# Attention items of a hybrid trunk: sample heads in pairs, past keys as stationary operand, five items ahead in place of three

## What is computed

```python
def sb_attend(q_pos, q, k, v, k_pos):
    z = jnp.einsum('bhqd,bhkd->bhqk', q, k) * (HEAD_DIM ** -0.5)
    mask = k_pos[None, :] < q_pos[:, None]
    log_skip = jnp.where(mask, jax.nn.log_sigmoid(-z), 0.0)
    later = lax.cumsum(log_skip, axis=3, reverse=True) - log_skip
    w = jnp.where(mask, jnp.exp(jax.nn.log_sigmoid(z) + later), 0.0)
    return jnp.einsum('bhqk,bhkd->bhqd', w, v)

def fox_attend(q_pos, q, fq, k, v, k_pos, fk):
    z = jnp.einsum('bhqd,bhkd->bhqk', q, k) * (HEAD_DIM ** -0.5)
    z = z + fq[..., :, None] - fk[..., None, :]
    z = jnp.where(k_pos[None, :] <= q_pos[:, None], z, -jnp.inf)
    return jnp.einsum('bhqk,bhkd->bhqd', jax.nn.softmax(z, axis=-1), v)
```

## Time and profile before

| | |
|---|---|
| median of 3 runs | 1691.65 us (1691.54 to 1693.9) |
| profiled execution | 1690.64 us |
| its span | 1688.5 us |
| PE busy over the span | 1509.1 us (89%) |
| DVE, ACT busy | 932.9 us (55%), 779.2 us (46%) |
| items stage, first to last matmul | 634 to 994 us |
| mean granted TensorE clock | 0.95 |

### The profile page before, as it was taken

How to read it: one execution, slowest core, us unless ns; L and a number is a source line. 1 busy time by engine, 2 the same in 40 slices (tenths; PEclk the granted TensorE clock), 3 DMA queues, 4 the chain that set the end, 5 groups by cost and what they waited for, 6 DMA issues and landing times. The chain is left out here.

```text
span 1688.5 us, 23869 instructions
## 1 busy us (share of the span) xinstructions
PE 1509.1 (89%) x8837; PEld 1343.5 (80%) x8837; DVE 932.9 (55%) x1169; ACT 779.2 (46%) x1109; POOL 187.4 (11%) x135
## 2 busy tenths in 40 slices
PE   5799999999999989999999989979964998999950
PEld 3479899999999978888999979967853876878840
DVE  7623012222323327777777744443246997999947
ACT  8422012113332327777777741121113776787733
POOL 0100000000000002000000001212103333432320
PEclk9899999999999999999999989989976999999985
DMA  7246344547656659776657223444316899999538
GB/s 282 82 128 193 110 141 145 168 150 218 205 186 184 213 174 233 186 200 152 152 126 178 72 101 106 162 146 162 113 50 200 249 335 300 261 280 288 105 53 323
DMA packets 233077, 300.14 MB, mean 178 GB/s; under 512 B 86441, under 2 KB 171537, under 8 KB 232954
## 3 DMA queue, kind: packets, MB, share of 16 engines
q1 hardware_dynamic: 223458, 264.01, 51.2%
q0 software_dynamic: 9504, 34.61, 8.5%
HBM read 264.23 MB, written 87.81 MB: 208 GB/s over the span
## 5 line engine op out<-in xcount | busy, mean ns | idle before, releaser
L773 PE MATMUL G<-hhi,proj_whi 128*128 128x384 f32 x768 | 178.5, 340 | 0.0
L773 PE MATMUL G<-hhi,proj_wlo 128*128 128x384 f32 x768 | 176.1, 337 | 0.0
L773 PE MATMUL G<-hlo,proj_whi 128*128 128x384 f32 x768 | 176.0, 337 | 0.0
L2005 DVE TENSOR_TENSOR experts_ulo<-plain,experts_uhi 128x2048 fp32r<-128x2048 f32 x66 | 150.8, 2285 | 18.9 <-issue 10.3
L1109 PE MATMUL G<-items_WT,items_vt 128*128 128x128 f32 x1152 | 150.6, 276 | 0.3
L1949 ACT ACTIVATE experts_uhi<-plain 128x2048 fp32r x66 | 126.6, 1920 | 33.8 <-PEq L80 23.4
L1109 PEld LDWEIGHTS G<-items_WT,items_vt 128*128 128x128 f32 x1152 | 139.4, 192 | 2.0 <-ACT items_WT L1162 2.0
L773 PEld LDWEIGHTS G<-hhi,proj_whi 128*128 128x128 f32 x768 | 136.0, 188 | 2.7 <-DVE proj_wlo L853 2.2
L773 PEld LDWEIGHTS G<-hhi,proj_wlo 128*128 128x128 f32 x768 | 137.8, 188 | 0.0
L773 PEld LDWEIGHTS G<-hlo,proj_whi 128*128 128x128 f32 x768 | 137.7, 188 | 0.0
L1906 PE MATMUL G<-experts_uhi,experts_ghi 128*128 128x512 f32 x264 | 109.0, 413 | 9.1 <-DVE experts_glo L2009 8.7
(11 more groups left out here) (314 smaller groups left out, 3157.9 us busy)
## 6 DMA issues: line engine op xcount, KB each, us to landing
plain<-in_w_dram SPq DMA_DIRECT2D x132, 512.0 KB
plain<-in_w_dram SPq DMA_DIRECT2D x33, 1024.0 KB
proj_wraw<-in_w_ada_dram SPq DMA_DIRECT2D x32, 512.0 KB
proj_wraw<-in_w_in_dram SPq DMA_DIRECT2D x20, 512.0 KB
qkhi_d<-proj_ohi SPq DMA_DIRECT2D x16, 576.0 KB, 2.8
qklo_d<-proj_olo SPq DMA_DIRECT2D x16, 576.0 KB, 3.0
gate_d<-proj_full SPq DMA_DIRECT2D x16, 576.0 KB, 3.8
merge_sg<-gate_d SPq DMA_DIRECT2D x16, 576.0 KB, 6.2
```

What stands on the lines that cost most here:

```text
L773: m = pe.matmul(G[:, g + c, 0:CH], w[r][:, k, :], a[:, k, c * CH:(c + 1) * CH], start=k == 0 and q == 0, stop=k == KD - 1 and q == 2)
L2005: dve.tensor_tensor(half(ulo[j], c), raw_up(side[n], c), half(uhi[j], c).bitcast(F32), ALU.subtract).then_inc(u_lo, 1)
```

## The change

Scores of the sample item's past part are turned round: each sequence's past keys `kc` are stationary and its queries move, high and low side by side in 32 columns, from a joint tensor `q` (`qs` in the code). That is eight matmuls and gives keys by queries, high and low apart. `add_past` on DVE adds the two into `zt` in two operations, and PE transposes `zt` into the slot (`turn_past`). `widen`, `qmhi` and `qmlo` are gone. Values of the sample item are computed once for two heads of the same kind: `take` writes both heads' weights to `W2`, and the second head's values handle 256 columns and 32 columns a sequence. `AHEAD` is 5, `S` has six buffers, `R` four, and y is split one item later. PE's first wait is for the first diagonal mask.

```diff
-                AHEAD = 3
+                AHEAD = 5
+                RING = 4
...
-                    pe.wait_ge(masks, FIRST_MASK)
+                    pe.wait_ge(masks, DIAGONAL)
...
                             for b in range(NB):
-                                for j, qm in enumerate((qmhi, qmlo)):
-                                    pe.matmul(G[:, g, 0:P], qm[:, b * P:(b + 1) * P], kc[f][:, b * PAST:(b + 1) * PAST],
-                                              start=b == 0 and j == 0, stop=b == NB - 1 and j == 1)
-                            m = part(G[:, g, P:2 * P], ks[f][:, SEQ:T], mnew[f])
-                        m.then_inc(z_ready, 1)
+                                new = slice(SEQ + b * NQ, SEQ + (b + 1) * NQ)
+                                m = pe.matmul(G[:, g + 1, b * 2 * NQ:(b + 1) * 2 * NQ], kc[f][:, b * PAST:(b + 1) * PAST], qs[f][:, :, new],
+                                              start=True, stop=True)
+                            m.then_inc(z_past, 1)
+                            part(G[:, g, P:2 * P], ks[f][:, SEQ:T], mnew[f])
+
+                    def turn_past(n):
+                        pe.wait_ge(z_summed, n // TT + 1)
+                        pe.transpose(G[:, slot(n), 0:P], zt[:], ident[:]).then_inc(z_ready, 1)
...
+                            out = G[:, 4 + y % 2, 0:2 * P]
+                            pe.matmul(out, vt[f][:, TT - 1, :], W2[f][:, 1].rearrange("p e n -> p (e n)"), start=True, stop=False)
+                            pair = out.rearrange("p (e n) -> p e n", e=2)
                             for b in range(NB):
-                                m = pe.matmul(out[:, b * NQ:(b + 1) * NQ], vc[f][:, b, :], w[:, 0, b * NQ:(b + 1) * NQ],
-                                              start=False, stop=b == NB - 1)
+                                new = slice(b * NQ, (b + 1) * NQ)
+                                m = pe.matmul(pair[:, :, new], vc[f][:, b, :], W2[f][:, 0, :, new], start=False, stop=b == NB - 1)
...
-                        if 0 <= i - 1 < NI:
+                        if 0 <= i - 1 < NI and has_pv(i - 1):
                             values(i - 1)
+                        if 0 <= i + AHEAD < NI and late(i + AHEAD):
+                            turn_past(i + AHEAD)
...
+                    def add_past(n):
+                        parts = G[:, slot(n) + 1, 0:2 * P].rearrange("p (b j i) -> p b j i", j=2, i=NQ)
+                        if n >= TT:
+                            dve.wait_ge(z_ready, n - TT + 1)
+                        dve.wait_ge(z_past, n // TT + 1)
+                        dve.tensor_copy(zt[:].rearrange("p (b i) -> p b i", i=NQ), parts[:, :, 0, :]).then_inc(z_first, 1)
+                        dve.wait_ge(z_first, n // TT + 1)
+                        dve.tensor_tensor(zt[:].rearrange("p (b i) -> p b i", i=NQ), parts[:, :, 1, :], zt[:].rearrange("p (b i) -> p b i", i=NQ),
+                                          ALU.add).then_inc(z_summed, 1)
...
+                    for i in range(-AHEAD, NI + 2):
+                        if 0 <= i + AHEAD < NI and late(i + AHEAD):
+                            add_past(i + AHEAD)
+                        if 0 <= i + AHEAD - 1 < NI and items[i + AHEAD - 1][0] == 0:
+                            stick(i + AHEAD - 1)
+                        if 0 <= i + AHEAD < NI and items[i + AHEAD][0] == 1 and not late(i + AHEAD):
+                            least(i + AHEAD)
+                        if 0 <= i + AHEAD - 1 < NI and items[i + AHEAD - 1][0] == 1:
+                            invert(i + AHEAD - 1)
+                        if 0 <= i + AHEAD < NI and items[i + AHEAD][0] == 1 and late(i + AHEAD):
+                            least(i + AHEAD)
+                        if 0 <= i - 2 < NI and y_last(i - 2):
+                            low_y(i - 2)
```

More of the change, by code:

```diff
@@ L1062, in part @@
                         def part(out, key, mask):
-                            pe.matmul(out, qhi[f][:, q], key, start=True, stop=False)
+                            pe.matmul(out, qs[f][:, 0, q], key, start=True, stop=False)
                             if mask is not None:
@@ new lines, in high_y @@
+                        for e in both if late(n) else (h % 2,):
+                            a, t0, w = slice(e * HD, (e + 1) * HD), t // 4 * 4, (t % 4 + 1) * P
+                            first = e * P if late(n) else 0
+                            act.activation(yhi[a, 4 * f + h // 2, t0 * P:t0 * P + w], G[a, 4 + y_use(n) % 2, first:first + w], ACT.Copy).then_inc(y_hi, 1)
+                    act.wait_ge(masks, FIRST_MASK)
+                    for i in range(-AHEAD, NI + 2):
+                        if 0 <= i + AHEAD - 1 < NI and items[i + AHEAD - 1][0] == 1:
+                            exponent(i + AHEAD - 1)
+                        if 0 <= i + AHEAD < NI and items[i + AHEAD][0] == 0 and not late(i + AHEAD):
+                            weigh(i + AHEAD)
@@ L1237, in _ @@
[L1237 to L1247 removed]
+                        dve.wait_ge(y_hi, y_done[y_use(n) + 1])
@@ new lines, in low_y @@
+                        for e in both if late(n) else (h % 2,):
+                            a, t0, w = slice(e * HD, (e + 1) * HD), t // 4 * 4, (t % 4 + 1) * P
+                            first = e * P if late(n) else 0
+                            dve.tensor_tensor(ylo[a, c, t0 * P:t0 * P + w], G[a, 4 + y_use(n) % 2, first:first + w],
+                                              yhi[a, c, t0 * P:t0 * P + w].bitcast(F32), ALU.subtract).then_inc(y_lo, 1)
+                    dve.wait_ge(masks, FIRST_MASK)
```

136 lines of the change are left out of this document (53 added, 83 removed).

## The result

The changed kernel takes 1720.26 us (median; 1717.12 to 1721.63), the kernel before 1692.49 on the same chip. The ratio is 1.0165 with a 95% interval of 1.0151 to 1.0179: slower by 28 us. The prediction said slower, 1706 in a range of 1668 to 1722. The direction was right, the size of the loss was about half of what came.

What follows compares the result with a forecast made beforehand. PE was taken to bound the kernel, with DVE and ACT no reserve. Five ahead was to lose the sample part's saving: 1690.6 + 14.7 for the heads + 1.0 to the median, rounded 1706 us, range 1668 to 1722.

Steps and rivals of the forecast that it cites:

- What bounds the kernel: Items stage: PE sets the pace, busy 325.2 of 332.6 us; DVE and ACT not full, but no reserve.
- Parts 1 and 2: Sample scores turned round and sample values paired on PE: 13.3 and 14.9 us saved, 28.2 if nothing else is late.
- Part 3: Small edits: copies and memsets hidden, add_past 0.55 us a head on DVE, earlier first scores under 1 us.
- Part 4, stick heads: Five ahead: PE waits for add_past's sum, a least and a take; 24.3 us, 24.9 with paired values, before 23.18.
- The walk: Round-by-round adding of PE, DVE and ACT steps through a head, giving PE's waits: 5.55 us in an unpaired stick head.
- Part 4, FoX heads: Five ahead: waits for add_past's sum and behind ACT's table load; 21.55 us, 22.85 with paired values, before 21.53.
- Head 0: Start of the loop, already DVE's chain, with add_past now in it: about +2 us (0 to 3).
- Head 15: Last head, no later scores and no table switch: 1.3 us saved.
- The sum: Heads 2 to 13 +12.5 us, head 14 +1.1, head 15 -1.3, head 0 +2, last y copies +0.4: +14.7.
- The signs: PE waits 1.5 to 3 us for add_past's sum in stick heads; wrong if under 1, or FoX heads average below 20.
- The saving arrives: Rival: PE's saving shows because DVE reaches add_past by 6.6 us; 1655 to 1687 us, chance 0.22.
- The clock falls too: Rival: PE's clock drops after its 2.6 us stand in stick heads; 1714 to 1722 us or beyond, chance 0.15.

Runs made afterwards that it cites:

- Kernel 1: Changed kernel with three items ahead, two R buffers and y one item later, so the new sample part alone: 1690.7 us, 0.9992 of the kernel before.
- kernel 6: Changed kernel with AHEAD 3, ACT's take ahead of the sigmoid's table load and its y copy first in the round: 1668.7 us, ratio 0.9861.
- kernel 3: Changed kernel, five ahead, with ACT copying y at the start of its round, not at its end: 1705.8 us, ratio 1.0101.
- kernel 4: Changed kernel with 12 unread PE transposes per stick head (28 in head 0) before the wait for add_past's sum: 1714.1 us, ratio 1.0131.
- kernel 7: Changed kernel, five ahead, with both ACT order changes (take before the sigmoid's table load, y copy first): 1698.0 us, ratio 1.0042.
- kernel 5: Kernel before with its old sample part, given only five ahead, four R buffers and the later y: 1720.7 us, ratio 1.0164.
- kernel 2: Changed kernel, five ahead, with ACT doing the take before the sigmoid's table load in a head's first item: 1706.6 us, ratio 1.0087.
- kernel 12: As kernel 6 (three ahead, both ACT order changes) but with two R buffers in place of four: 1667.9 us, ratio 0.9850.
- kernel 9: Kernel 6 with the pairing undone, each head's sample values computed apart: 1678.2 us, ratio 0.9915.

## Why the prediction was right or wrong, step by step

**What bounds the kernel.** PE set the pace before, and DVE and ACT are no reserve: held. Kernel 1 shows it best: 17.7 us less busy time on PE, as much more waiting, and no time gained.

**Parts 1 and 2.** Eight matmuls of 32 columns appear as x8 with 1.04 us including the tail and 0.89 to the next row (787.53 to 788.42 in head 6), 0.111 from start to start where 0.107 were taken; the sum of PE's work without waits, 18.77 a FoX head, was measured as 18.9 (kernel 6). Paired values 2.15 and not 2.0. Sizes right within 0.2 us a head.

**Part 3.** `add_past` was taken at 0.55 us: COPY 0.28 and the sum 0.29, 0.53 from the start of the first (791.67) to the start of the next scan (792.20). Right. PE's first wait, for the mask, is 8.2 us in place of 9.2.

**Part 4, stick heads.** Forecast 24.3 and 24.9, measured 24.31 and 25.28. The walk's places are all there: the sum last, then the least at item 2 of the next head, then the take behind the exponent. Their sizes are not those of the walk: 0.59 + 0.41 + 2.14 = 3.14 in place of 4.05 up to the sum, 0.73 in place of 1.05, 0.36 in place of 0.45: 4.23 in all where the walk had 5.55. PE's busy time made up for it: 20.07 us in this head by the first row below (the stretch of head 6), where 18.77 were taken. So the exact 24.31 is luck: two errors of 1.3 us cancel. Why PE is busy longer for the same work when it stops in between is not shown; the row's duration is longer than the step from one start to the next, and behind each stop that tail is counted too.

```profile
780.20:804.50 24.30, 20.07 (x157) 17.55 (x156) 17.71 (x29) 16.82 (x34) 0.00 (x0) 1.00 0.44 105
804.50:828.20 23.70, 21.39 (x175) 19.59 (x174) 16.10 (x36) 16.24 (x37) 0.00 (x0) 1.00 0.66 160
```

**Part 4, FoX heads.** Forecast 21.55 and 22.85, measured 21.91 and 23.71. The waits of the second are 23.7 - 21.39 = 2.3 us in all (second row), against 2.05 forecast; the busy time is 21.4 against 20.8. This is a term of the walk that was mis-sized, and more in PE's work than in its waits: 0.86 a head, with the 0.36 of the other FoX head and the 0.38 of the paired stick head 1.6 in four heads, 4.8 in heads 2 to 13.

**The clock.** Here the prediction failed as a sum. It saw the drop in a row, priced it (4 heads x 2.4, up to 10), and gave it a chance of 0.15 as a rival, with nothing for it in the forecast, when it comes on top of the forecast. The heads in which the clock fell are 4, 10, 11 and 13; they were 0.69, 1.28, 1.61 and 1.63 us longer than their like, 5.2 in all. Of head 4's 0.69, 0.35 is not the clock's: kernels 3, 4 and 7, granted 1.00 there, have head 4 longer than head 8 by the same 0.35. That leaves 4.9 for the clock, and in kernel 4, with the wait filled, it is gone. The rival put the drops into stick heads, behind the wait for the sum; two of the four came in FoX heads, behind the wait of 1.84 for a take. The busy table around the drops in head 10 and in head 13:

```profile
885.00:890.00 5.00, 2.86 (x17) 2.67 (x16) 4.90 (x6) 1.50 (x5) 0.00 (x0) 0.68 0.13 31
890.00:895.00 5.00, 5.00 (x30) 4.80 (x30) 3.67 (x10) 3.99 (x10) 0.00 (x0) 0.64 1.02 240
...
960.00:965.00 5.00, 2.62 (x22) 2.20 (x21) 3.16 (x11) 4.09 (x10) 0.00 (x0) 1.00 0.53 127
965.00:970.00 5.00, 4.88 (x28) 4.73 (x29) 2.05 (x5) 2.81 (x9) 0.00 (x0) 0.66 1.01 234
```

**Head 0.** This is another step that failed. The prediction gave it +2 us (0 to 3); it was +5.2 (the values of item 7 start at 662.35 in place of 657.11). PE stood 3.2 us for the sum and then ran at about half clock:

```profile
649.22 0.48 PE L1093 MATMUL G<-all_ident,items_zt 128*128 128x128 f32 x1 [3.21 <-DVE items_zt L1203]
```

```profile
650.00:655.00 5.00, 5.00 (x26) 4.91 (x26) 4.41 (x9) 3.03 (x8) 0.00 (x0) 0.53 1.10 284
```

It is a matter of the lookahead and not of the sample part: with the old sample part and five ahead head 0 is even later (kernel 5, +6.9), with the new one and three ahead it is earlier than before (kernel 6, 656.0).

**Head 15** was to save 1.3 us and took 20.1, 0.3 less than the 20.4 of before. The prediction gave it one sentence and no walk, and 1.0 us was missed.

**The sum.** Forecast up to head 15's item 7: 2 + 12.5 + 1.1 - 1.3 = 14.3. Measured 29.15. The missing 14.85: clock 4.9, the sizes of the FoX and paired heads 4.8, head 0 3.2, head 15 1.0, head 1 0.4, what head 4 has beside the clock 0.35, and 0.2 of rounding. The forecast's own mechanism, heads too long by the two waits, is shown by kernels 2, 3 and 7. What failed is the sum: it kept to what undisturbed heads in the middle cost, sized four of them at 93.6 where 95.2 were measured, gave head 0 +2 where +5.2 came, and had nothing for the clock, which took 4.9.

**The signs.** PE's wait for the sum was to be 1.5 to 3 us in stick heads and under 1.2 in FoX heads; it was 2.14, 1.27 in stick heads with paired values (0.70 in head 4, where the clock had fallen), and 0.47 to 0.65 in FoX heads. The wait for items_mx was to be about 1 and was 0.73. Neither of the two signs of being wrong came.

**The rivals.** "The saving arrives" is excluded for this kernel, and right for kernel 12, which gets to 1667.9: it needs DVE to reach the sum in time, as the rival said, and gets that from ACT's y copy done first and from three ahead. "The clock falls too", 1714 to 1722, contains 1720.3, but by luck: the clock did fall, and cost 4.9 us, which would make 1711 of 1706; the other 9 us come from the other terms above.

At the two places where the Trainium skill was weighed, the runs go with this case's rows. By the 81 ns that the Trainium skill gives for a pair of weight load and 128-column matmul (TensorE: Matmul & The Clock Gate, Back-to-back issue gap) the removed sample scores would have been worth, as an estimate, 0.51 us a head less than by this case's 0.113. The FoX head of pure work, forecast at 18.77 by 0.113 and 19.28 by the smaller price, took 18.95 in kernel 6, so the trace's price is the nearer one. The drain of about 1380 ns that the Trainium skill puts beside a table load (ScalarE: Activation LUTs, What ACT_TABLE_LOAD costs) is again not there: in FoX head 5 of the changed kernel the load starts at 769.41 and the sigmoid behind it at 770.71 (ACT in order of time), 1.30 us.

```profile
769.41 1.28 ACT L1151 ACT_TABLE_LOAD   x1
770.71 0.28 ACT L1151 ACTIVATE items_R<-G 128x128 f32<-128x128 f32 x1
```

**What stays open.** Why the clock fell in head 10 and not in head 6, which has the same wait of 2.14 us at the same place, no run tells. That the stick heads with three ahead are limited by DVE (19.5 of 21.5 us busy) is read from the busy table and was not tested by taking work from DVE. The two order changes were never tried on the kernel before, with its old sample part, so how much of kernel 12's 24 us needs the new sample part is not known beyond the 9.5 us of kernel 9.

## What to carry to other kernels

When PE waits for a second engine at one place, look at which rounds the lookahead puts side by side before deepening it: five ahead laid the largest sticks on DVE beside the shortest rounds on PE, and with its buffers and the later y cost 29 us on the old sample part and, `AHEAD` alone, 34 us on the new one, while with three ahead four R buffers gave nothing over two. A saving on the engine that sets the pace can turn into waits for the others: here the sample part was worth nothing alone, and the two moves of a line on ACT then gave 18 us. In a sum from one undisturbed period, price the start of the loop and the clock separately and add them; a wait of 2 us in a PE that is otherwise full cost 1.3 to 1.6 us more where the clock fell behind it.

## What the runs showed of the hardware that was not expected

- The granted clock fell at single waits of 1.84 to 2.14 us between busy stretches: in head 11 the turn at 916.28 waited 1.84 and 915 to 920 has 0.75, in head 13 the turn at 965.12 waited 1.84 and 965 to 970 has 0.66. The same wait in other heads (1.83 at 771.79, 2.14 at 792.33) left it at 1.00. In head 4 it fell when PE had just waited 0.47 us: the values below took 1.51 us, where the same row in head 8, with the same wait, took 0.94, and 745 to 750 has 0.50. With twelve small transposes ahead of the wait in the stick heads only, one drop was left after 660 us, in stick head 12 (0.66 from 935 to 940), and none in a FoX head.

```profile
743.21 1.51 PE L1119 MATMUL G<-items_WT,items_vt 128*128 128x128 f32 x6 [0.47 <-ACT items_WT L1170]
```

- A low clock need not cost time: kernel 4's head 12 had 0.66 for five of its microseconds and was as long as head 8 at 1.00 (25.31 and 25.30 us).
- A 256-column pass of the 32-bit values costs 0.21 us, twice that of 128 columns, whereas 128, 32 and 16 columns all cost 0.104 to 0.113.
- A PE that is stopped and started shows a longer busy time for the same work: 18.9 us in an unbroken head without paired values (kernel 6), 20.1 in one with five waits (head 6 of the changed kernel).
